# The second attention in two groups of 256 queries, the later one in steps between the expert picks

## What is computed

```python
def attend(qn, qr, kn, kr, v):       # 16 heads, 512 queries, 768 keys (512 tokens + 256 of context)
    s = jnp.einsum('bqhd,bkhd->bhqk', qn, kn) + jnp.einsum('bqhd,bkd->bhqk', qr, kr)
    p = jax.nn.softmax(s.astype(jnp.float32) * ATTN_SCALE, axis=-1).astype(v.dtype)
    return jnp.einsum('bhqk,bkhd->bqhd', p, v)
...
    return (g[..., :D_MODEL] * y_a + g[..., D_MODEL:] * y_c) @ w_out      # y_a from the attention, y_c from the convolution
...
def peer_ffn(h, w_pq, sub_keys, u_tab, v_tab):
        q = (xc @ w_pq).reshape(P_CHUNK, P_HEADS, 2, P_DK // 2)
        s = jnp.einsum('thpd,hpkd->thpk', q, sub_keys)
        ...                                                     # top 16 of the 16 x 16 best pairs: 16 experts per head
        act = jax.nn.gelu(jnp.einsum('thkd,td->thk', u_tab[expert], xc), approximate=False)
        return jnp.einsum('thk,thkd->td', gate * act, v_tab[expert])
```

## Time and profile before

| | before |
|---|---|
| median of 3 runs | 3005.24 us |
| profiled execution, time and span | 3017.8 us, 3016.5 us |
| PE busy | 2650.2 us, 88% |
| DVE busy | 1575.2 us, 52% |
| ACT busy | 655.1 us, 22% |
| moved from memory | 698.40 MB |
| attention (1265.3 to 1499.3) | 234.0 us |
| first tile, until PE has the scores of its first routing (to 1554.2) | 54.9 us |
| picks, from the first gelu (1586.3) on | 1430.2 us |

### The profile page before, as it was taken

One profiled execution on the slowest core, in us unless ns is written; L12 is line 12 of the kernel. 1 busy time (PEld: TensorE's weight loads), 2 busy tenths in 40 slices (PEclk: granted clock), 3 DMA queues, 4 the chain that ended last, 5 costly groups with the idle time before them and its releaser, 6 DMA issues.

```text
span 3016.5 us, 24185 instructions
## 1 busy us (share of the span) xinstructions
PE 2650.2 (88%) x8458; PEld 1407.6 (47%) x8458; DVE 1575.2 (52%) x3526; ACT 655.1 (22%) x1591; POOL 561.5 (19%) x523
## 2 busy tenths in 40 slices
PE   8998899999998999899988788897998777777776
PEld 3684446666444444356664345443553323232222
DVE  1106335443106991266636655668466676758554
ACT  2114220001001002256511121123112221222111
POOL 0000000000000000000003333434434444434332
PEclk9996799999999999999998999998999999999999
DMA  3220023343221221000259999999999999999997
GB/s 137 99 84 1 22 84 139 140 167 125 91 77 64 84 79 49 14 1 12 86 222 403 379 357 409 392 396 384 400 379 391 390 419 420 420 420 420 420 420 314
DMA packets 88312, 702.07 MB, mean 233 GB/s; under 512 B 10089, under 2 KB 10729, under 8 KB 12929
## 3 DMA queue, kind: packets, MB, share of 16 engines
q0 software_dynamic: 73728, 536.90, 44.0%
q1 hardware_dynamic: 12416, 158.60, 13.6%
q10 hardware_dynamic: 2048, 5.03, 0.5%
HBM read 698.40 MB, written 2.10 MB: 232 GB/s over the span
## 4 chain that ended last, share of the span: by engine, by line
PE 61%; DMA 23%; DVE 10%; ACT 3%; issue 1%; POOL 0%; ACTq 0%; DVEq 0%; POOLq 0%
PE psum L346 33%; PE psum L895 12%; DMA weights<-in_experts,expert 12%; DMA slot<-in_experts,expert 11%; PE psum L739 3%; DVE slot L1832 2%; PE psum L684 2%; PE psum L828 2%; DVE weights L1832 2%; PE psum L761 1%; PE psum L812 1%; PE psum L747 1%; PE psum L797 1%; ACT spare_row L1289 1%; PE psum L520 1%
## 5 line engine op out<-in xcount | busy, mean ns | idle before, releaser
L895 PE MATMUL psum<-slot,spare_row 128*128 128x512 f32 x1096 | 530.4, 630 | 141.2 <-ACT spare_row L1289 141.0
L895 PE MATMUL psum<-weights,spare_row 128*128 128x512 f32 x952 | 452.8, 620 | 134.2 <-ACT spare_row L1289 134.1
L1832 DVE CUSTOM_DVE_ANT_0 slot<-slot,hT 128x1024 f32<-128x1024 f32 x274 | 332.9, 1223 | 228.8 <-DMA slot<-in_experts,expert 227.9
L346 PE MATMUL psum<-xnT,weights 128*128 128x257 f32 (+2 forms) x1568 | 423.8, 432 | 2.8 <-DVE xnT L1338 2.8
L895 PEld LDWEIGHTS psum<-slot,spare_row 128*128 128x128 f32 x1096 | 211.1, 200 | 428.3 <-issue 220.3
L1832 DVE CUSTOM_DVE_ANT_0 weights<-weights,hT 128x1024 f32<-128x1024 f32 x238 | 289.6, 1223 | 199.5 <-DMA weights<-in_experts,expert 198.9
L1886 POOL DMA_INDIRECT weights<-in_experts,expert x238 | 258.8, 1087 | 710.5 <-PE psum L895 373.9
L1886 POOL DMA_INDIRECT slot<-in_experts,expert x274 | 299.5, 1093 | 472.2 <-PE psum L895 457.8
L895 PEld LDWEIGHTS psum<-weights,spare_row 128*128 128x128 f32 x952 | 178.8, 196 | 388.6 <-issue 202.7
L346 PEld LDWEIGHTS psum<-xnT,weights 128*128 128x128 f32 x1568 | 298.7, 191 | 118.5 <-issue 82.2
L1284 ACT ACTIVATE coef<-hidden 128x2 f32<-128x2 f32 (+1 forms) x257 | 52.3, 203 | 1059.4 <-DVE hidden L1832 1059.4
(11 more groups left out here) (320 smaller groups left out, 2554.8 us busy)
## 6 DMA issues: line engine op xcount, KB each, us to landing
weights<-in_w_mod SPq DMA_DIRECT2D x12, 2048.0 KB, 8.4
weights<-in_w_pq SPq DMA_DIRECT2D x12, 2048.0 KB, 12.0
weights<-in_w_up SPq DMA_DIRECT2D x11, 2048.0 KB, 7.7
weights<-in_w_out SPq DMA_DIRECT2D x8, 2048.0 KB, 10.5
weights<-in_w_in SPq DMA_DIRECT2D x8, 2048.0 KB, 8.2
weights<-in_w_o_mla SPq DMA_DIRECT2D x6, 2048.0 KB, 9.7
weights<-in_w_in_t SPq DMA_DIRECT2D x4, 2048.0 KB, 10.8
weights<-in_w_down SPq DMA_DIRECT2D x4, 2048.0 KB, 7.6
```

Of the source, the lines that this page charges most:

```text
L346: last = pe.matmul(out, lhsT, rhs, start=start and n == 0, stop=stop and n == len(pairs) - 1)
L895: last = pe.matmul(acc.pair[:, half, :], k.diags[pick % 8], k.slots[slot][:, D + half * 512:D + (half + 1) * 512], start=h0 == 0 and j == ...
L1832: ins = dve.tensor_tensor_reduce(slot[:, 0:D], slot[:, 0:D], k.h2[:, i, :], 1.0, 0.0, ALU.mult, ALU.add, hid[:, j:j + 1])
```

## The change

The attention's generator now takes a group g of two tiles. Group 0 (tiles 0 and 1, 32 items) runs ahead of the picks as before; group 1 (tiles 2 and 3) runs as `late` steps, one item a step, 42 steps in all, and the dense part of tiles 2 and 3 behind it (74 steps). The dense part of tiles 0 and 1 is done together ahead of the picks. The values are projected for each pair of heads in the loop (`value_rows`), since no room is left for those of all heads; keys and value rows are thus computed twice, once a group. The rotated copy of the queries comes out of the projection (the weights hold the swapped columns too), instead of a product with a permutation. Four buffers of 1 MB (half of x, of the gates, of the merged branch, and two rows of the modulation) are written to DRAM and read back ahead of dense(1), since the attention of the picks lies in their room. There are six slots up to pick 352 instead of 256.

```diff
-    def attention():
-        unit_q, wq = weights(2, 1536)
+    def attention(g):
+
+        my, items = k.work[g], k.heads_order[g]
+        unit_q, wq = weights(2, 2048)
...
+        def value_rows(p):
+            u = take(("v", g, p), n=2)
+            for j in range(KT):
+                last = pe.matmul(u.pair[:, j // 3, (j % 3) * P:(j % 3 + 1) * P], my.ckv[:, j * P:(j + 1) * P], wkv[:, 0, D + p * P:D + (p + 1) * P],
+                                 start=True, stop=True)
             last.then_inc(u.fill())
...
-        for c in range(AH * NT + 4):
-            if c < AH * NT:
-                h, i = k.heads_order[c]
+        for c in range(len(items) + 4):
+            if c >= 4 and c % 4 == 3:
+                u = values((c - 4) // 4)
+            if 0 <= c - 3 < len(items):
+                transposes(c - 3)
+            if c < len(items):
+                h, i = items[c]
                 scores(c)
-                if i == 1 and h % 4 == 3 and h + 1 < AH:
-                    queries(h // 4 + 1)
-                if i == 1 and h % 2 == 1 and h + 1 < AH:
+                if c % 4 == 1 and h + 2 < AH:
                     keys(h // 2 + 1)
-            if 0 <= c - 3 < AH * NT:
-                transposes(c - 3)
-            if c >= 4 and c % 4 == 3:
-                u = values((c - 4) // 8, (c - 4) // 4 % 2)
+                if c % 4 == 2 and h // 4 + 1 < AH // 4:
+                    queries(h // 4 + 1, (0, 1) if c % 8 == 2 else (2, 3))
+            if c >= 4 and c % 4 == 0:
+                value_rows(c // 4 - 1)
+            yield
...
     def peer():
-        late = chained(dense(1), dense(2))
+        late = chained(attention(1), dense(1))
...
+    def hold(name, ready, sem):
+        act.wait_ge(*ready)
+        act.dma_start(k.hold[name], k.later[name]).then_inc(sem, 16)
...
+    def back(name, out, sem):
+        sp.wait_ge(out, 16)
+        sp.dma_start(k.later[name], k.hold[name]).then_inc(sem, 16)
...
+        if g:
+            sp.wait_ge(*k.psum.of["q", 1, AH // 4 - 1, 3].free)
+            sp.wait_ge(*k.psum.of["a_v", 1, AH // 2 - 1].full[-1])
+            back("merged", s.hold_merged, s.back_merged)
+            back("sig", s.hold_sig, s.back_sig)
+            back("x", s.hold_x, s.back_x)
+            back("rows", s.hold_rows, s.back_rows)
...
-        return 8 if b in (2, 4) else 3 if self.finishes(b) else 0
+        return 13 if b == 4 else 3 if self.finishes(b) else 0
...
-        k.late = [[0], [1], [2, 3]]
+        k.late = [[0, 1], [2, 3]]
...
-            slot = pick % 6 if pick < 2 * PH * TOPK else (pick - 2 * PH * TOPK) % 10
+            slot = pick % 6 if pick < NARROW else (pick - NARROW) % 10
```

More of the change, by code:

```diff
@@ L170, in steps @@
     def steps(self, b):
-        return 2 if self.picks(b) < 4 * TOPK or b in (2, 4) else 1
+        return 2 if self.picks(b) < 4 * TOPK or b == 4 else 1
     def finishes(self, b):
@@ L715, in queries @@
                 k.ring_done[unit_q] = u.full[-1]
-            v = take(("q_swap", g))
-            pe.wait_ge(*u.free)
-            pe.matmul(v.pair[:, 0, :], k.swap2, k.turn[0], start=True, stop=True).then_inc(v.fill())
         def keys(p):
-            u = take(("k", p), n=2)
+            u = take(("k", g, p), n=2)
             for a in range(2):
-                last = chain(u.pair[:, a, 0:KH], [(wkv[:, 0, p * P:(p + 1) * P], k.ckv[:, a * KH:(a + 1) * KH])])
+                last = chain(u.pair[:, a, 0:KH], [(wkv[:, 0, p * P:(p + 1) * P], my.ckv[:, a * KH:(a + 1) * KH])])
@@ L914, in tensor_program @@
     conv_out()
-    attention()
+    for _ in attention(0):
+        pass
     first_tile()
@@ L1158, in conv_out, with attention, queries @@
         feature_norm("n_ckv_c", [k.ckv[:, SEQ:NKV]], CTX, 128, 3, k.feature_root[2])
-    def attention():
-        act.wait_ge(*of["pw", KC - 1].free)
-        for j in range(KT):
-            u = of["values2", j]
-            for half in range(2):
-                act.wait_ge(*u.full[half])
-                ins = act.activation(k.values[j][:, half * 512:(half + 1) * 512], u.pair[:, half, :], ACT.Copy)
-            ins.then_inc(u.out)
-        def queries(g):
-            Q = k.Q[g % 2]
+    def attention(g):
+        my, items = k.work[g], k.heads_order[g]
+        if g == 0:
+            hold("merged", of["pw", KC - 1].free, s.hold_merged)
+        else:
+            act.wait_ge(s.hold_rows, 16)
+            act.wait_ge(s.hold_sig, 16)
+            act.wait_ge(s.merged, KC)
+            act.wait_ge(s.h2, 2)
+        def queries(q):
@@ L1203, in attention @@
         queries(0)
+        yield
         keys(0)
-        for c in range(AH * NT + 4):
-            if c < AH * NT:
-                h, i = k.heads_order[c]
+        yield
+        yield from k.gap(2)
+        for c in range(len(items) + 4):
+            if c < len(items):
+                h, i = items[c]
                 exps(c)
-                if i == 1 and h % 4 == 3 and h + 1 < AH:
+                if c % 4 == 1 and h + 2 < AH:
+                    keys(h // 2 + 1)
+                if c % 8 == 2 and h // 4 + 1 < AH // 4:
@@ L1222, in rows @@
             copy_out(("row", i), halves(k.mod_rows[i]), of["row", i].pair)
+            if i == 1:
+                hold("rows", of["row", i].free, s.hold_rows)
+        act.wait_ge(s.hold_merged, 16)
+        act.dma_start(k.work[1].rope, A["rope2"][:, :, PAIR:SEQ]).then_inc(s.ld_rope2, 16)
         act.wait_ge(s.gain2, 1)
-        load(k.final[:], "final_g", s.ld_final2)
     def dense(g):
@@ L1249, in route @@
             copy_out(("route", b, u_), k.scores[:, 4 * u_:4 * u_ + 4, :].rearrange("p r k -> p (r k)"), of["route", b, u_].pair[:, 0, :])
-        for _ in range(12):
+        for _ in range(12 + (k.steps(b - 1) if b else 0)):
             yield
@@ L1597, in feature_norm, with query_norm @@
         ins.then_inc(s.feature)
+    def query_norm():
+        root = k.feature_root[0]
+        dve.wait_ge(*of["n_cq"].free)
+        dve.reciprocal(root[:], root[:]).then_inc(v.up())
+        dve.wait_ge(*v.now())
+        dve.wait_ge(s.hold_x, 16)
+        for x in range(2):
+            for g in range(2):
+                cut = slice(g * PAIR, (g + 1) * PAIR)
+                ins = dve.scalar_tensor_tensor(k.work[g].cq[:, x, :], k.cq[:, x, cut], col(k, "q_g", x), root[:, cut], ALU.mult, ALU.mult)
+        ins.then_inc(s.feature)
     def conv_out():
```

334 lines of the change are left out of this document (189 added, 145 removed).

## The result

The changed kernel takes 3099.11 us (median of 4 runs, 3094.52 to 3102.98), the kernel before 3004.28 in the same comparison (4 runs). The ratio is 1.030, 95% interval 1.0276 to 1.0324. The profiled execution took 3094.52 against 3017.8: +76.7, where I had forecast +64.

What follows compares the result with a forecast made beforehand. PE bounds the attention and DMA the picks; after the change, waits for banks bind both attentions. -66 + 34 + 88 + 0 + 8 = +64 on the profiled 3017.8 gives 3082, or 3069 on the median's scale; range 2985 to 3120.

Steps and rivals of the forecast that it cites:

- waits in both attentions: Likeliest case: waits for banks bind ahead of the picks and beside them; 3069 us, chance 0.57 for 3035 to 3100.
- The first attention, -66: Attention ahead of the picks: half its items leave, PE then waits for ACT's copies; 168 us instead of 234.0.
- the blocks of 4.4, 6.0 and 7.85: First attention: us between ends of scores to the second, third and fourth item; with 1.95 to the first, 20.2.
- The first tiles, +34: Dense part ahead of the picks: merge +13.2, `w_out` +13.75, query columns +4.3, another turn and norm +2.8.
- The first 42 groups, +88: First picks, with the late attention beside them: 362 us instead of 273.6, including PE coming 10 late.
- copy done, transposes, scores, row maximum, table load, exponential, copy: Attention beside the picks: loop through three bank pairs, about 6.35 us for a plain item, 7.8 on average.
- those of the slots: First 42 groups: loop of the six gather slots, 24.6 us for three groups, 8.2 each, taken as 8.3.
- Behind them, 0 and +8: Later picks: 0 for the 74 groups including the 4 MB read back, +8 for six slots in 48 more groups.
- The waits don't bind: Rival: PE's work alone counts in both attentions; -34, 2971 us, chance 0.10.
- DMA sets the picks: Rival: the first 42 groups carry fewer weights and go faster, 222 us; -76 overall, 2929 us, chance 0.03.
- Only the first attention is bound by the waits: Rival: beside the picks PE's work sets the time instead; 0 overall, 3005 us, chance 0.15.
- The drain at each table switch: Rival: beside the picks, two further ACT stalls of 1.38 in 32 items; +88, 3157 us, chance 0.03.

Runs made afterwards that it cites:

- experiment 3: On the changed kernel, DVE copies the result of `values` ahead of that step's row maximum and weights; ratio 1.0222 to the kernel before.
- Experiment 1: The run of `order_both`, PE's steps reordered in both attentions of the changed kernel; ratio 1.0012 to the kernel before.
- `order_both`: Changed kernel with PE's steps in both attentions reordered: scores and projections, transposes of three items earlier, value rows, `values` last; ratio 1.0012 to the kernel before.
- `late_first`: `order_both` with DVE taking each group's attention or dense step ahead of the routing steps; ratio 0.9952 to the kernel before.
- experiment 10: The kernel before with one number changed, six gather slots until pick 352 instead of 256; ratio 1.0003.

## Why the prediction was right, and where it was not

The time (3099 for 3069, within 2985 to 3120) and the direction were right. The likeliest case, waits in both attentions, is the one that happened. The sum was 12.7 us short, less than its terms were off: the first attention by 24 one way, the 42 groups with what stands ahead of them by 10 the other way (24 in the groups themselves, and 14 back), and the two stretches behind by 5 one way and 6 the other. That these partly cancelled is luck.

- **The first attention, -66, was -42.** The waits that the order would bring stand in the trace where the blocks of 4.4, 6.0 and 7.85 put them. For those behind ACT's copies I had 5.2 in each block of four, 36 in seven, and 33.2 were measured. Two things were missing. The step "to the first: transposes and scores, 1.95" has a wait of its own: scores take the bank of the last `values`, whose copy stands behind the maximum and the weights on DVE, 11.4 in all (experiment 3). And I priced PE's own work at 2.4 GHz because it had run so; I had written that PE would be busy some 120 us, and it was 144.7. Experiment 1 separates the two: 121.4 us for the same work once the waits are gone. My start and drain were too long, at 14 beside the 120, and this hid a part of it: "PE alone would take 134", and `order_both` took 126.5.
- **The first tiles, +34**: +34.3, and for the reasons given: PE's busy time rose from 46.6 to 83.1. The merge took 27.8 (27.5 in my sum, though "64 passes" and "2 x 1.73" are half of what that needs), the product with `w_out` 27.5.
- **The first 42 groups, +88, were +64, with +14 ahead of them: 78.** I had PE come 10 late to the picks and the first gelu at 31. ACT has its exponential of the first routing and the first gelu behind the copies of the last query columns, so the gelu itself was late: 46.4. In the 36 groups I had 322, and they took 303.0. What was too dear is the loop "copy done, transposes, scores, row maximum, table load, exponential, copy" with every link in it. By itself, the load was worth 20 us in 36 groups and not 46; PE's order 18; and the routing steps ahead of the maximum 17.6, for which I had counted 27. There are two loops, one through PE and one through DVE and ACT. Opening both (`late_first`) brought 40.1, little more than the 18.1 and 17.6 of opening each alone, and the table load lay in the second. Two of my lengths were also more than their printed terms: those of a plain item add up to 6.26 and not 6.35, those of the slots to 23.2 for three groups and not 24.6, which is 7.7 a group and not 8.2. At 7.7 for both loops, the 14 groups for which I took 8.3 would be some 8 us less by my own terms.
- **Behind them, 0 and +8**: +5.3 and +2.1. My 0 for the read back is not borne out: the 74 groups take 436.1 and 432.1 us in the two kernels without it, and 439.6 to 446.3 in the nine kernels that read back just ahead of them and keep one step in each group. DMA moved 174.6 MB there instead of 169.8. A cost of some 4 to 14 us stands, and no run tells how much of it is the read back. For the six slots I had a reason (nothing is spare where DVE has a step of 2.09) but no wait; experiment 10 shows none in the kernel before.
- **The rivals.** "The waits don't bind" fell in the first attention, with 47 us of idle time. "DMA sets the picks" fell with a DMA share of 0.71. "Only the first attention is bound by the waits" fell too, since the same new order brings 18 us beside the picks. The drain at each table switch, which the Trainium skill's page "ScalarE: Activation LUTs" gives in its section "What ACT_TABLE_LOAD costs", would be, by an estimate from that page's figure, 1.38 at each of the 60 switches that the exponentials bring to the 36 groups, 83 us. Taking these switches out gave 20 with the loads, which alone are 77 us of ACT's time. The rows, too, have 0.02 between load and exponential (1695.74 + 1.28 to 1697.04), as the earlier trace rows had.

The order explains why a change that takes half the attention off the front of the kernel was slower: 73 of the 77 us between the profiled spans go with it. With PE's steps in another order it is level with the kernel before, and with DVE's exchanged as well it is 0.5% faster.

## What to carry to other kernels

Where buffers are handed out in rotation, the order in which an engine takes them is a schedule. For each take write down who read that buffer last and what stands ahead of that reader on its engine; with four pairs and twelve takes to a block this was a list of twelve lines, and it was worth some 80 us of 3099. When work is put beside a pipelined loop, look for engines that take turns within one round: the new work that the other engine waits for belongs ahead of work that nobody there waits for, so that the other can start.

An engine with idle time is no promise of room: in groups 6 to 42 PE's, DVE's and DMA's shares were 85%, 67% and 71% in the changed kernel, and exchanging steps without removing any brought 40 us.

## What I had not expected of the hardware

Waits came with a lower clock, and so cost more than their length. In the first attention of the changed kernel PE was idle for 47.2 us and the granted clock was 0.88; with the wait for DVE's copy gone (42.1 idle) it was 0.93; with 5.1 idle it was 1.00. The same products were busy for 144.7, 134.6 and 121.4 us. For the 42 us of waiting that the new order took away, 23 more came back by the clock.

In the last 140 groups, with DMA at 1.00, the kernel before didn't notice four slots fewer in 48 of them (ratio 1.0003, 0.9986 to 1.002).
